# A hybrid encoder trunk on one core: memory attention's softmax weights transposed by VectorE in 32x32 blocks and through HBM instead of by TensorE

## The reference

```python
def _memory_attention(q, mem, w_kv):
    km, vm = jnp.split(mem @ w_kv, 2, axis=-1)
    q = q.reshape(b, s, XATTN_HEADS, XATTN_HD) * (XATTN_HD ** -0.5)
    ...
    logits = jnp.einsum('bshd,bmhd->bhsm', q, km).astype(jnp.float32)
    probs = jax.nn.softmax(logits, axis=-1).astype(vm.dtype)
    return jnp.einsum('bhsm,bmhd->bshd', probs, vm).reshape(b, s, XATTN_W)
```

## Time and profile before

| | |
|---|---|
| median of 3 runs | 1245.52 us (1245.37 to 1245.91) |
| span of the profiled execution, first to last instruction | 1244.7 us; what lies around the span is in the runs' times only |
| TensorE busy | 1235.2 us (99%), 7370 matmuls; granted clock 0.998 of full speed on average |
| VectorE busy | 1024.4 us (82%) |
| ScalarE busy | 730.3 us (59%) |
| DMA engines | 55.5% for the stream's queue, 227 MB read |

### The profile page before, as it was taken

The page is one execution under the profiler, slowest core; times in us unless marked ns, Lnnn a source line. Parts: engine busy times, 40 slices in busy tenths (PEclk is TensorE's granted clock), DMA queues, the critical chain, the costliest instruction groups (busy, mean ns, idle before and its releaser), DMA issues.

```text
span 1244.7 us, 19689 instructions
## 1 busy us (share of the span) xinstructions
PE 1235.2 (99%) x7370; PEld 1082.9 (87%) x7370; DVE 1024.4 (82%) x1599; ACT 730.3 (59%) x1190; POOL 20.1 (2%) x29
## 2 busy tenths in 40 slices
PE   9999999999999999999999999999999999999997
PEld 7988888888999988888889888888888888888886
DVE  5876888889779888988887978988888776988887
ACT  6675765555766546555555546655554774755552
POOL 0001000000000100000000000000000001000000
PEclk9999999999999999999999999999999999999999
DMA  9834576554553345655655764656554533666651
GB/s 333 285 120 136 190 248 190 186 192 163 175 182 119 122 150 169 227 187 195 201 173 168 233 204 162 227 195 199 190 186 169 187 119 119 218 207 201 196 190 54
DMA packets 64539, 229.27 MB, mean 184 GB/s; under 512 B 7575, under 2 KB 9239, under 8 KB 63421
## 3 DMA queue, kind: packets, MB, share of 16 engines
q1 hardware_dynamic: 64444, 228.02, 55.5%
HBM read 226.93 MB, written 1.06 MB: 183 GB/s over the span
## 4 chain that ended last, share of the span: by engine, by line
PE 97%; DMA 1%; SPq 1%; DVE 0%; issue 0%; ACT 0%; DVEq 0%
PE pair L768 28%; PE acc L862 21%; PE pair L771 14%; PE pair L800 4%; PE pair L801 4%; PE pair L802 4%; PE acc L768 2%; PE acc L843 2%; PE acc L842 2%; PE acc L841 2%; PE pair L1022 2%; DMA raw<-in_stream 1%; PE pair L825 1%; PE pair L827 1%; PE pair L829 1%; PE acc L931 1%
## 5 line engine op out<-in xcount | busy, mean ns | idle before, releaser
L1278 DVE TENSOR_TENSOR w_lo<-raw,w_hi 128x1024 fp32r<-128x1024 f32 x400 | 482.6, 1221 | 105.3 <-ACT w_hi L1040 103.7
L1040 ACT ACTIVATE w_hi<-raw 128x1024 fp32r<-128x1024 f32 x400 | 420.5, 1058 | 213.2 <-PE pair L771 70.8
L768 PE MATMUL pair<-xT,w_hi 128*128 128x512 f32 x1520 | 477.8, 396 | 0.0
L771 PEld LDWEIGHTS pair<-xT,w_lo 128*128 128x128 f32 x1520 | 285.5, 188 | 67.2
L771 PE MATMUL pair<-xT,w_lo 128*128 128x256 f32 x1520 | 298.6, 278 | 0.0
L768 PEld LDWEIGHTS pair<-xT,w_hi 128*128 128x128 f32 x1520 | 233.8, 189 | 3.2 <-issue 0.3
L1087 ACT ACTIVATE hid<-pair 128x512 f32<-128x512 f32 x88 | 52.6, 597 | 124.9 <-PE pair L771 124.9
L1319 DVE TENSOR_TENSOR hid<-pair,hid 128x512 f32<-128x512 f32 x88 | 60.7, 690 | 47.9 <-ACT hid L1087 47.7
L800 PE MATMUL pair<-xT,w_hi 128*128 128x256 f32 x336 | 97.8, 291 | 0.0
L801 PE MATMUL pair<-xT,w_hi 128*128 128x256 f32 x336 | 95.0, 283 | 0.0
L802 PE MATMUL pair<-xT,w_lo 128*128 128x256 f32 x336 | 94.9, 283 | 0.0
(11 more groups left out here) (223 smaller groups left out, 1661.9 us busy)
## 6 DMA issues: line engine op xcount, KB each, us to landing
raw<-in_stream SPq DMA_DIRECT2D x400, 512.0 KB, 4.6
gains<-in_ln SPq DMA_DIRECT2D x8, 1024.0 KB, 8.4
bias<-bias_scratch SPq DMA_DIRECT2D x2, 1152.0 KB, 9.0
raw<-in_stream SPq DMA_DIRECT2D x8, 256.0 KB, 6.6
x_tok<-in_x_t SPq DMA_DIRECT2D x4, 256.0 KB, 6.2
y_tok<-in_mem_t SPq DMA_DIRECT2D x2, 512.0 KB, 7.1
x_tok<-in_x SPq DMA_DIRECT2D x1, 1024.0 KB, 6.5
out<-x_tok SPq DMA_DIRECT2D x4, 256.0 KB, 2.0
```

What stands on the lines that cost most here:

```text
L768: pe.matmul(bank, w_hi[:, slot, kk * P:(kk + 1) * P], xT[:, kk].rearrange("p a s -> p (a s)"), start=(kk == 0), stop=(kk == KT - 1), skip_ ...
L771: last = pe.matmul(bank[:, 0:SEQ], w_lo[:, slot, kk * P:(kk + 1) * P], xT[:, kk, 0, :], start=False, stop=(kk == KT - 1), skip_group_check ...
L1040: nc.scalar.activation(w_hi[:, u % SPLIT, :], raw[:, u % RAW, :], ACT.Copy).then_inc(hi_ready, 1)
L1278: v.tensor_tensor(w_lo[:, u % SPLIT, :], raw[:, u % RAW, :], w_hi[:, u % SPLIT, :].bitcast(F32), ALU.subtract).then_inc(lo_ready, 1)
```

## The change

The constant `SWAPPED` is 0, so the heads of the differential attention keep their transposes on TensorE (`turnw`), and the items `swap`, `fetch` and `spread` are left out. For memory attention the item `xturn` is gone on TensorE and ScalarE, and there are two new ones. `xswap` on VectorE transposes the 128x1024 weights of a head pair in blocks of 32x32 into the buffer of the exponentials, and SyncE stores that to a scratch tensor in HBM by four DMAs of 32 partitions each. `xfetch` on SyncE waits for the four stores and loads the blocks back in transposed order by one DMA. `xpv` waits for its landing and reads the blocks by a pattern of runs of 32 elements. The places: in the attention layers `xpv` stood at h = 7 and 9 and stands at 9 and 11 (in layer 0 each of these h is 4 higher, as before); in the HGRN layer it stood at 5 and 7, in the conv layer at 5 and 9, and stands at 9 and 11 in both. In the HGRN layer the multiplication by the reciprocals (`xprob`) goes from VectorE to ScalarE, as four Copy operations of 128x256 for each head pair, with a scale for each row. SyncE now walks the list of items too: a unit's load is issued at the item `lo` of the unit five before it, so that stores and fetches take their place between the loads.

```diff
+SWAPPED = 0
...
-            at = {0: [it("xlog", 0), it("xlog", 1)], 1: [it("xexp", 0)], 2: [it("xexp", 1), it("xprob", 0)],
-                  3: [it("xprob", 1)], 5: [it("log", 0), it("log", 1)],
-                  6: [it("exp", 0), it("xturn", 0)], 7: [it("exp", 1), it("xpv", 0)],
-                  8: [it("prob", 0), it("xturn", 1)], 9: [it("prob", 1), it("xpv", 1), it("log", 2), it("log", 3), it("turnw", 0)],
...
+            at = {0: [it("xlog", 0), it("xlog", 1)], 1: [it("xexp", 0)], 2: [it("xexp", 1), it("xprob", 0), it("xswap", 0)],
+                  3: [it("xprob", 1), it("xswap", 1), it("xfetch", 0), it("xfetch", 1)],
+                  5: [it("log", 0), it("log", 1)], 6: [it("exp", 0)], 7: [it("exp", 1)],
...
+            if not SWAPPED:
+                at[9] = [it("prob", 1), it("xpv", 0), it("log", 2), it("log", 3), it("turnw", 0)]
+                at[11] = [it("turnw", 1), it("exp", 3), it("prob", 2), it("xpv", 1)]
...
         elif kind == "conv":
...
-            at = {0: [it("xlog", 0), it("xexp", 0), it("xlog", 1), it("xexp", 1)], 1: [it("xprob", 0), it("xprob", 1)],
-                  4: [it("xturn", 0)], 5: [it("xpv", 0)], 8: [it("xturn", 1)], 9: [it("xpv", 1)]}
+            at = {0: [it("xlog", 0), it("xexp", 0), it("xlog", 1), it("xexp", 1)],
+                  1: [it("xprob", 0), it("xswap", 0), it("xprob", 1), it("xswap", 1)],
+                  2: [it("xfetch", 0), it("xfetch", 1)], 9: [it("xpv", 0)], 11: [it("xpv", 1)]}
...
         else:
...
-                  4: [it("xturn", 0)], 5: [it("xpv", 0)], 6: [it("xturn", 1)], 7: [it("xpv", 1)]}
+                  2: [it("xswap", 0), it("xswap", 1), it("xfetch", 0), it("xfetch", 1)],
+                  9: [it("xpv", 0)], 11: [it("xpv", 1)]}
...
+        def swap_source(n):
+
+            s = n % 2
+            return (ex[:, s] if items[prob_pos[n]][0] == "xprob" else prob[:, s, 1:2]).rearrange("p i t s -> p (i t s)")
+
+        def swap_target(n):
+
+            name, layer, h = items[prob_pos[n]]
+            if name == "prob":
+                place = a_sq[:, 1 + h % 2]
+            elif h:
+                place = xprobT[:]
+            elif layer_kind(layer) == "attn":
+                place = probT[:, 4:6].rearrange("p h t k s -> p (h t k s)")
+            else:
+                place = prob[:, 0].rearrange("p i t s -> p (i t s)")
+            return place.rearrange("p (a e) -> p a e", a=4)
...
+            for item in items:
+                name = item[0]
+                if name == "begin" and item[1] % 2:
+                    next_unit(item[1] // 2 * 2 + item[2] + RAW)
+                elif name == "lo":
+                    next_unit(item[1] + RAW)
+                elif name in ("xswap", "swap"):
+                    n = weights_of(item)
+                    sp.wait_ge(swapped, swap_ord[n])
+                    for a in range(4):
+                        rows = slice(32 * a, 32 * a + 32)
+                        sp.dma_start(swap_scratch[n][a].rearrange("b i e -> i b e"), swap_source(n)[rows].rearrange(
+                            "i (b e) -> i b e", b=4)).then_inc(swap_stored[n % 2], 16)
+                elif name in ("xfetch", "fetch"):
...
+                    sp.wait_ge(swap_stored[n % 2], 64 * swap_count[n])
+                    sp.dma_start(swap_target(n), swap_scratch[n].rearrange("a b i e -> (b i) a e")).then_inc(swap_landed[n % 2], 16)
...
-                elif name == "xturn":
-
-                    n = prob_ord[pos]
...
-                    for i in range(2):
-                        bank = side(pos, i)
-                        for k in range(2):
-                            for t in range(TT):
-                                last = pe.transpose(bank[:, k * SEQ + t * P:k * SEQ + (t + 1) * P],
-                                                    prob[:, n % 2, i, t, k * P:(k + 1) * P], ident[:])
-                        last.then_inc(xprob_turned, 1)
...
-                    pe.wait_ge(xprobT_ready, 2 * u + 2)
+                    n = weights_of(item)
+                    pe.wait_ge(swap_landed[n % 2], 16 * swap_count[n])
                     pe.wait_ge(vm_ready, layer + 1)
                     bank = side(pos)
+                    weights = swap_target(n).rearrange("p a (i t k j) -> p i k t a j", i=2, t=2, k=2)
...
                     if n >= 2 and logit_name[n - 2] == "xlog":
-                        act.wait_ge(xprob_ready, logit_name[:n - 1].count("xlog"))
+                        act.wait_ge(swap_stored[n % 2], 64 * swap_count[n - 2])
...
-                elif name == "xturn":
-                    u = ordinal[pos]
+                elif name == "xprob" and layer_kind(item[1]) == "hgrn":
+                    n = weights_of(("xswap",) + item[1:])
+                    act.wait_ge(inv_ready, item[2] + 1)
                     for i in range(2):
-                        act.wait_ge(xprob_turned, 2 * u + i + 1)
-                        if u >= 1:
-                            act.wait_ge(xpv_done, u)
-                        nc.scalar.activation(xprobT[:, i], side_bank(pos, i)[:].rearrange(
-                            "p (k s) -> p k s", k=2), ACT.Copy).then_inc(xprobT_ready, 1)
+                        for t in range(TT):
+                            j = 2 * i + t
+                            last = nc.scalar.activation(prob[:, n % 2, i, t, :], ex[:, n % 2, i, t, :], ACT.Copy,
+                                                        scale=row_inv[:, n % 2, j:j + 1])
+                    last.then_inc(xprob_ready, 1)
...
+                elif name in ("xswap", "swap"):
+                    n = weights_of(item)
+                    of = prob[:, n % 2] if name == "xswap" else prob[:, n % 2, 0:1]
+                    if name == "xswap" and layer_kind(item[1]) == "hgrn":
+                        dve.wait_ge(xprob_ready, item[2] + 1)
+                    v.transpose(swap_source(n).rearrange("p (b c j) -> p c b j", b=4, j=32),
+                                of.rearrange("p i t (k b j) -> p (i t k) b j", k=2, j=32)).then_inc(swapped, 1)
```

More of the change, by code:

```diff
@@ L132, in make_schedule @@
                   19: [it("pv", 4), it("pv", 5), it("ms", 1), it("tok", 1), it("ms", 2)], 20: [it("scale", 1), it("tok", 2)],
                   21: [it("scale", 2)]}
+            if not SWAPPED:
+                at[9] = [it("prob", 1), it("xpv", 0), it("log", 2), it("log", 3), it("turnw", 0)]
+                at[11] = [it("turnw", 1), it("exp", 3), it("prob", 2), it("xpv", 1)]
+                at[13].insert(0, it("turnw", 2))
+                at[15].insert(0, it("turnw", 3))
+                at = {h: [i for i in row if i[0] not in ("swap", "fetch", "spread")] for h, row in at.items()}
@@ L270, in trunk_kernel, with weights_of @@
     logits_of = {item[1]: logit_ord[pos] + 1 for pos, item in enumerate(items) if pos in logit_ord}
[L271 to L274, removed]
+    prob_pos = [pos for pos, i in enumerate(items) if i[0] in ("xprob", "prob")]
+    prob_ord = {(items[pos][0][:-4],) + items[pos][1:]: n for n, pos in enumerate(prob_pos)}
+    swap_count, swap_ord, turned_ord, seen = {}, {}, {}, {}
+    for item in items:
+        if item[0] in ("xswap", "swap"):
+            n = prob_ord[("x" if item[0][0] == "x" else "",) + item[1:]]
+            swap_count[n] = seen[n % 2] = seen.get(n % 2, 0) + 1
+            swap_ord[n] = len(swap_ord) + 1
+        elif item[0] == "turnw":
+            n = prob_ord["", item[1], item[2]]
+            turned_ord[n] = len(turned_ord) + 1
+    def weights_of(item):
+        return prob_ord[("x" if item[0][0] == "x" else "",) + item[1:]]
     EARLY_TURNS = {(m, 1) for m in range(2 * DEPTH - 1)}
@@ L293, in trunk_kernel @@
             banks = ()
-        elif name in ("turn", "xturn"):
+        elif name == "turn":
             banks = (0, 1)
@@ L502, in trunk_kernel @@
         scratch = nc.dram_tensor("bias_scratch", [HEADS, 512], F32, kind="Internal").ap()
+        swap_scratch = [nc.dram_tensor(f"swap_scratch{n}", [4, 4, 32, 256 if items[pos][0] == "xprob" else 128], F32, kind="Internal").ap()
+                        for n, pos in enumerate(prob_pos)]
         out_dram = out.rearrange("b (t p) d -> p (b t) d", p=P)
@@ L1525, in _ @@
                 elif name in ("xprob", "prob"):
-                    n = prob_ord[pos]
+                    n = weights_of((name.replace("prob", "swap"),) + item[1:])
                     s = n % 2
```

106 lines of the change are left out of this document (68 added, 38 removed).

## The result

The changed kernel took 1251.38 us (median of 4 runs, 1250.25 to 1253.1), the kernel before 1245.72 us beside it: 1.0044 times as long, with an interval of 1.0031 to 1.0056. It is slower by 5.7 us by the medians and 5.5 by the ratio, more than the 2.5 us that a measurement can tell from no change. Run again in five rounds it took 1251.13 us against 1245.84 us, a ratio of 1.0045 (1.0032 to 1.0057). The forecast was 1246.4 us, no change, with a range up to 1252.0. The range holds the time; the point is 5 us short, and the kind of result was missed (no change was forecast, and it is slower).

The account below looks back on a forecast made before the run. TensorE, with 97% of the chain that ended last, was taken to bound the kernel. Terms -7.7 + 3.5 + 4.4 + 0.7 = +0.9 us on 1245.5 gave 1246.4 us, no change; range 1242.5 to 1252.0.

Parts of the forecast that it names:

- The four waits: TensorE waits 3.5 us before CG 2, 4.4 in the HGRN layer at two places, 0.7 in layer 0.
- The swap: Each of eight VectorE block transposes of 128x1024 float32 takes 1.22 us, 1.26 with its new wait.
- the rival of 2.4 us: Block transposes on VectorE cost twice a multiplication of the same tile, giving 1253.7 us; 9 in 100.
- What leaves TensorE: Eight transposes items, two in each layer, leave TensorE at 0.97 us each, 7.7 us in all.
- The bound on strided reading: Moved products reading weights in runs of 32 could cost up to 2.4 us for all eight; nothing was taken.
- TensorE's clock: Clock may fall in the two long waits, slowing half chunks behind: 1249.3 us, up to 1252 for both; 13 in 100.
- the fourth rival: TensorE's clock falls in a long wait (HGRN or conv layer), +3 us for one; 13 in 100.
- its signs of being wrong: The two long waits missing, or ending with a landing, or half chunks behind them running at the lower clock.
- SyncE's queue: 40 added DMAs hold it some 6 us per swap pair, counted as nothing; as rival late weights, 1250.4 us, 8 in 100.
- Time around the span: Whole execution: 0.8 us lie around the profiled span of 1244.7 us and stay there.

Follow-up runs that it names:

- the filled kernel: Changed kernel with unread matmuls added on TensorE, 14 before the HGRN layer's first level product and 12 before CG 2; 1248.09 us, ratio 1.0018.
- the eased kernel: Changed kernel with HGRN normalisation back on VectorE, HGRN's first product earlier, conv normalisation and swaps behind CG 1's product and CB 0; 1244.74 us, ratio 0.9991.
- the last experiment: The eased kernel with the conv layer as in the kernel before (TensorE transposes, no swap there); 1243.09 us, ratio 0.9972 to the kernel before.

## Why the prediction came out as it did

**The four waits: right.** Places, releasers and lengths: 3.4 us before CG 2 (3.5 foretold), 0.7 + 3.6 = 4.3 us in the HGRN layer (4.4), 0.7 in layer 0 (0.7), none in layer 3. In sum 8.4 us where 8.6 were written. Their causes stood the tests: without swaps the conv wait fell by 2.0 us, layer 0's went, and the HGRN wait did not fall at all; without Copies the latter fell by 2.0.

**The swap: right.** 1.25 us on all eight, against 1.22, and the rival of 2.4 us fell. No row had shown such an operation, so the 1.22 was a guess between bounds of 0.6 and 1.47 us that came out well. The Trainium skill's 311 ns for a 128x128 transpose in blocks (VectorE: DVE Perf Modes, The three transpose paths) is given for 16-bit elements; eight times it would be an estimated 2.5 us, and the measured 1.25 us for eight such tiles of 32-bit elements is half. The Trainium skill's advice (VectorE: DVE Perf Modes, Rules for kernel authors) to use TensorE for a 128x128 transpose came out right in the conv layer, where VectorE has no room, and not in the attention layers, which gained 0.9 and 1.7 us without it.

**What leaves TensorE: 7.7 us was too much.** By layer 3 it is 0.86 us an item, 6.9 us for eight. A half chunk behind a small item is longer than one behind a half chunk (in the kernel before 695.04 to 697.96 us is 2.92 us, 700.75 to 703.53 is 2.78). The 0.97 took the shorter one. It is 0.8 us of the miss. The bound on strided reading (2.4 us) was not needed.

**TensorE's clock: the term that failed.** The forecast had it at nothing; it stood as the fourth rival with 13 in 100 and a price of 3 us for one wait and up to 1252 us for both. The prediction had named it among its signs of being wrong (the half chunks behind the waits at the lower clock), and this sign came. Filling the two waits took away 3.0 us (1251.13 to 1248.09). The sum is then: before 1245.84 - 6.9 + 8.4 + 3.0 = 1250.3 us against 1251.13 measured. Without the clock it is 1247.3 against the filled kernel's 1248.09. The last 0.8 us lie in both. Most of it shows in how much later TensorE's items start. A wait costs some 0.2 us more than its bracket says: in the eased kernel the three waits of 0.44, 0.23 and 0.83 us put TensorE back by 0.68, 0.46 and 1.07. And the moved products cost 1.20 to 1.26 us at their new places, where the one ahead of the first level product had cost 1.0.

The reasoning for its small chance was that the clock stood at 1.0 in all work. But the row that spoke for it was quoted: where TensorE had nothing, the level fell. The forecast wrote two idle stretches of 3.5 and 4 us into a kernel that had none, and gave the known effect of idleness a small chance. The price of 3 us for one wait was too high: 3.0 us is what both cost together in the median, and one cost 1.5 to 2.7 us in profiled executions (5.35 and 6.56 us for 3.87) and another nothing. That the range nevertheless held the time is owed to its upper end, which had been set wide for the rivals, and not to the forecast's own terms, whose range ended at 1249.0. The Trainium skill's rule (TensorE: Matmul & The Clock Gate, Part 1) that idleness throttles the array is borne out. The Trainium skill also remarks there that one and the same kernel has different numbers of matmuls at the lower level in different runs, which it says of a kernel's start; here two executions differ so behind a wait (of 3.4 us before CG 2).

**SyncE's queue: right for this kernel.** In the HGRN layer it was held from 338.79 to 345.04 us, 6.3 us where 6 were written, and the stores landed after 2.3 us. The load of unit 116 landed at 352.8 us (about 352 foretold), and its rounding began there, with the first level product at 352.76. ScalarE's waits for weight units grew from 8.0 to 32.4 us in all (19.9 in the other execution), and none of TensorE's waits ends with one. GpSimd's queue, meant as the test of this term, did not settle it; it rests on these traces. It was hidden by the longer wait beside it, as the last experiment shows, and not free: 0.3 and 1.1 us in the two traces where that wait is gone, 0.4 in the one where it was 1.64.

**Time around the span.** I took 0.8 us from the one profiled execution and the median. Every later run of either kernel that lists both has 1.7 us or more (in the first rounds 1243.5 to 1244.5 us of span for 1245.3 to 1246.3 of the kernel before), so the profiled execution of before, with a span of 1244.7 us, was probably itself some 0.7 us longer than most. It cancels in the difference and moved nothing.

## What to carry to other kernels

Where a forecast writes an idle stretch like these (3.4 to 3.6 us) into a kernel whose TensorE hardly idled, the work at half speed behind it (0 to 2.7 us here, 1.5 in the middle) belongs into the sum and not among the rivals. When work leaves the bounding engine, its earlier arrival eats cover at every later meeting, so a wait appears even where nothing else was delayed; subtract it before blaming the added work. Take such a change layer by layer: here the two attention layers gain 0.9 and 1.7 us, the HGRN layer nothing or 1.0 once it is eased, and the conv layer, whose receiving engine is full, loses some 2.0.

## What was not expected of the hardware

Added, unread matmuls made the kernel 3.0 us faster. The same wait was followed by no slow stretch in one execution and by one in the next, and equal waits of 3.64 us by stretches that cost 1.5 and 2.7 us. DMAs issued by GpSimd in place of SyncE made the fetch leave 6 us behind its last store, and cost 21 and 32 us for 40 DMAs. A block transpose of 128x1024 float32 took 1245 to 1247 ns all eight times, about the time of a multiplication of the same tile (1.22 us).
